# Four RMSNorms of a hybrid SSD/attention trunk: broadcasting 1/rms by a repeated column, scale-and-shift on ScalarE

## What is computed

```python
def rmsnorm(x, w):
    y = xf * lax.rsqrt(jnp.mean(xf * xf, axis=-1, keepdims=True) + EPS)
    return (y * w.astype(jnp.float32)).astype(x.dtype)

def modulate(h, shift, scale):
    return h * (1 + scale) + shift

a_lat = modulate(rmsnorm(x_lat, norm1_w[i]), sh1, sc1)
a_ctx = modulate(rmsnorm(x_ctx, norm1_w[i]), csh1, csc1)
```

## Time and profile before

| | |
|---|---|
| median of 3 runs | 1397.04 us (1394.56 to 1397.6) |
| the profiled execution, first to last instruction | 1395.9 us |
| TensorE busy (matmul) | 1232.0 us, 88%, 7274 instructions |
| TensorE weight load | 743.7 us, 53% |
| VectorE busy | 928.7 us, 67%, 1445 instructions |
| ScalarE busy | 581.8 us, 42%, 1005 instructions |
| GpSimd busy | 116.5 us, 8% |
| HBM read | 171.22 MB, 123 GB/s over the span |
| bodies of the norms n=0, 2, 3, 4 | from 44.7, 613.7, 973.3 and 1205.1 us, together about 64 us |

### The profile page before, as it was taken

One profiled execution on the slowest core, in us unless ns is written; L12 is line 12 of the kernel. 1 busy time (PEld: TensorE's weight loads), 2 busy tenths in 40 slices (PEclk: granted clock), 3 DMA queues, 4 the chain that ended last, 5 costly groups with the idle time before them and its releaser, 6 DMA issues.

```text
span 1395.9 us, 20639 instructions
## 1 busy us (share of the span) xinstructions
PE 1232.0 (88%) x7274; PEld 743.7 (53%) x7274; DVE 928.7 (67%) x1445; ACT 581.8 (42%) x1005; POOL 116.5 (8%) x127
## 2 busy tenths in 40 slices
PE   7679988988988768969999999997999977799997
PEld 7335554554554543424444444443765535688886
DVE  5984674674665568988788788564527755755654
ACT  2344543553653434323433333222334544456642
POOL 0003024014015110000000000000000000000000
PEclk9989989989989969979999999998999997899998
DMA  9213102202202033634564554522222100355552
GB/s 391 89 56 106 61 16 92 73 15 79 86 31 91 1 121 112 225 145 181 183 238 183 187 227 155 218 85 89 91 91 91 60 30 31 122 212 207 181 196 106
DMA packets 24957, 172.88 MB, mean 124 GB/s; under 512 B 2768, under 2 KB 2768, under 8 KB 6608
## 3 DMA queue, kind: packets, MB, share of 16 engines
q1 hardware_dynamic: 19008, 129.28, 25.4%
q0 software_dynamic: 5184, 37.75, 7.4%
q10 hardware_dynamic: 720, 5.24, 1.0%
HBM read 171.22 MB, written 1.05 MB: 123 GB/s over the span
## 4 chain that ended last, share of the span: by engine, by line
PE 49%; DVE 10%; issue 2%; ACT 2%; DMA 0%; DVEq 0%; ACTq 0%; POOL 0%; SPq 0%
PE bank L1284 14%; PE bank L1285 14%; PE bank L1286 14%; PE bank L1569 1%; DVE arena L756 1%; DVE arena L803 1%; PE bank L1583 1%; DVE arena L798 1%; PE bank L1556 1%; PE bank L1558 1%; PE bank L1557 1%; ACT wh L390 1%; DVE arena L1014 1%; DVE hl L794 1%; PE bank L1576 1%
## 5 line engine op out<-in xcount | busy, mean ns | idle before, releaser
L1284 PE MATMUL bank<-hh,wh 128*128 128x512 f16 (+1 forms) x1152 | 399.8, 347 | 38.4 <-DVE hl L794 19.3
L726 DVE SCALAR_TENSOR_TENSOR wl<-raw,wh 128x1024 f16<-128x1024 f32 (+1 forms) x232 | 269.0, 1177 | 237.5 <-ACT wh L390 235.5
L1285 PE MATMUL bank<-hl,wh 128*128 128x512 f16 (+1 forms) x1152 | 399.2, 347 | 0.0
L1286 PE MATMUL bank<-hh,wl 128*128 128x512 f16 (+1 forms) x1152 | 398.8, 346 | 0.0
L390 ACT ACTIVATE wh<-raw 128x1024 f16<-128x1024 f32 (+1 forms) x232 | 229.9, 1011 | 288.8 <-PE bank L1286 219.1
L1284 PEld LDWEIGHTS bank<-hh,wh 128*128 128x128 f16 x1152 | 114.8, 100 | 147.8 <-issue 62.0
L1284 PE MATMUL bank<-arena,wh 128*128 128x512 f16 (+1 forms) x544 | 182.0, 335 | 10.9 <-DVE wl L726 3.8
L1285 PE MATMUL bank<-arena,wh 128*128 128x512 f16 (+1 forms) x544 | 181.9, 334 | 0.0
L1286 PE MATMUL bank<-arena,wl 128*128 128x512 f16 (+1 forms) x544 | 181.8, 334 | 0.0
L756 DVE SCALAR_TENSOR_TENSOR arena<-arena,araw 128x1024 bf16<-128x1024 f32 x144 | 167.6, 1219 | 0.2
L1286 PEld LDWEIGHTS bank<-hh,wl 128*128 128x128 f16 x1152 | 114.3, 99 | 95.7 <-issue 6.6
(11 more groups left out here) (194 smaller groups left out, 1451.5 us busy)
## 6 DMA issues: line engine op xcount, KB each, us to landing
raw<-wgu SPq DMA_DIRECT2D x44, 1024.0 KB, 4.8
arena<-wadaT POOLq DMA_DIRECT2D x36, 1024.0 KB, 5.1
raw<-wdn SPq DMA_DIRECT2D x16, 896.0 KB, 4.6
raw<-wxg SPq DMA_DIRECT2D x8, 1024.0 KB, 4.8
raw<-wz SPq DMA_DIRECT2D x8, 1024.0 KB, 4.8
raw<-wout SPq DMA_DIRECT2D x8, 1024.0 KB, 4.8
raw<-wdn SPq DMA_DIRECT2D x8, 1024.0 KB, 4.8
raw<-wqk SPq DMA_DIRECT2D x8, 1024.0 KB, 4.8
```

Source lines behind the costliest of these rows:

```text
L726: ve.scalar_tensor_tensor(wl[:, u.slot, a:b], raw[:, u.slot, a:b], WS, wh[:, u.slot, a:b], ALU.mult, ALU.subtract).then_inc(lo_done, 1)
L1284: pe.matmul(o, wh[:, u.slot, wsl], ahi[:, k, t0:t1], start=st, stop=False)
L1285: pe.matmul(o, wh[:, u.slot, wsl], alo[:, k, t0:t1], start=False, stop=False)
L1286: i = pe.matmul(o, wl[:, u.slot, wsl], ahi[:, k, t0:t1], start=False, stop=en)
```

## The change

Four things are changed.

1. `bcast` multiplies, for each block of 128 tokens, the column of `rt` repeated 128 times (as the weights) with the identity. The result is the same: 1/rms of each token on all partitions. It waits for c_rr; the matrices `rdg`, the semaphore c_dg and the product on VectorE are gone. `acc` keeps the memory.
2. `root` first issues a Sqrt of one element (eps into an unused column), ahead of its wait for the sums.
3. The scale-and-shift is issued by ScalarE as `Identity` with the columns wsc and wsh as scale and bias, for chunk k ahead of the rounding of chunk k-1. VectorE keeps the multiply for chunk k and the subtraction, which is now for chunk k-2.
4. In n=1 VectorE's small product for the gate column stands ahead of the reciprocal instead of behind it.

```diff
             def root(n, width, cs):
 
+                act.activation(small[:, 1:2], eps, ACT.Sqrt)
                 act.wait_ge(c_ss, n + 1)
                 act.activation(rt[:, cs:4], OB[0][:, cs:4], ACT.Sqrt, scale=1.0 / width, bias=eps).then_inc(c_rt, 1)
...
             def h_hi(n, t0):
 
-                for k in range(KC):
-                    act.wait_ge(n32_ok, HN[n] * KC + k + 1)
-                    act.activation(hh[:, k, t0:T], n32[:, k % 2, t0:T], ACT.Copy).then_inc(hh_ok, 1)
+                m = HN[n] * KC
+                kinds = [(0, 0, TC), (1, TC, T)][t0 // TC:]
+                for k in range(KC + 1):
+                    if k < KC:
+                        act.wait_ge(nt_ok, m + k + 1)
+                        if k >= 2:
+                            act.wait_ge(h_ok, m + k - 1)
+                        for b, a, e in kinds:
+                            i = act.activation(n32[:, k % 2, a:e], nt[:, k % 2, a:e], ACT.Identity, scale=wsc[:, k, b:b + 1],
+                                               bias=wsh[:, k, b:b + 1])
+                        i.then_inc(n32_ok, 1)
+                    if k:
+                        act.wait_ge(n32_ok, m + k)
+                        act.activation(hh[:, k - 1, t0:T], n32[:, (k - 1) % 2, t0:T], ACT.Copy).then_inc(hh_ok, 1)
...
                 ve.reciprocal(rt[:, cs:4], rt[:, cs:4]).then_inc(c_rr, 1)
-                ve.wait_ge(c_rr, n + 1)
-                ve.tensor_tensor(rdg[:, cs * P:T].rearrange("p (c l) -> p c l", l=P),
-                                 ident[:, None, :].to_broadcast([P, 4 - cs, P]),
-                                 rt[:, cs:4][:, :, None].to_broadcast([P, 4 - cs, P]), ALU.mult).then_inc(c_dg, 1)
...
             def h_lo(n, t0):
...
                 ve.wait_ge(c_bc, n + 1)
-                for k in range(KC):
-                    ve.tensor_tensor(nt[:, k % 2, t0:T], x[:, k, t0:T], OB[1][:, t0:T], ALU.mult).then_inc(nt_ok, 1)
-                    ve.wait_ge(nt_ok, m + k + 1)
+                for k in range(KC + 2):
+                    if k < KC:
+                        if k >= 2:
+                            ve.wait_ge(n32_ok, m + k - 1)
+                        ve.tensor_tensor(nt[:, k % 2, t0:T], x[:, k, t0:T], OB[1][:, t0:T], ALU.mult).then_inc(nt_ok, 1)
                     if k >= 2:
-                        ve.wait_ge(h_ok, m + k - 1)
-                    for b, a, e in kinds:
-                        i = ve.tensor_scalar(n32[:, k % 2, a:e], nt[:, k % 2, a:e], wsc[:, k, b:b + 1], wsh[:, k, b:b + 1],
-                                             ALU.mult, ALU.add)
-                    i.then_inc(n32_ok, 1)
-                    if k:
-                        lo(k - 1)
-                lo(KC - 1)
+                        ve.wait_ge(hh_ok, m + k - 1)
+                        ve.tensor_tensor(hl[:, k - 2, t0:T], n32[:, k % 2, t0:T], hh[:, k - 2, t0:T], ALU.subtract).then_inc(h_ok, 1)
...
-            inverse(1, 0)
             gw = small[:, 16:32]
             step(ve.tensor_scalar(gw, cc("gnw"), AS, None, ALU.mult))
+            inverse(1, 0)
...
             def bcast(n, cs):
 
-                pe.wait_ge(c_dg, n + 1)
-                pe.matmul(OB[1][:, cs * P:T], ones, rdg[:, cs * P:T], start=True, stop=True).then_inc(c_bc, 1)
+                pe.wait_ge(c_rr, n + 1)
+                for c in range(cs, 4):
+                    i = pe.matmul(OB[1][:, c * P:(c + 1) * P], rt[:, c:c + 1].to_broadcast([P, P]), ident, start=True, stop=True)
+                i.then_inc(c_bc, 1)
```

More of the change, by code:

```diff
@@ L157, in build @@
         n32 = carve(2 * T).rearrange("p (b t) -> p b t", b=2)
-        rdg = carve(T)
+        acc = carve(T)
         mark = at[0]
@@ L170, in build @@
         pre = carve(2 * 520).rearrange("p (b s t) -> p b s t", b=2, s=2)
-        acc = rdg
         xbc = carve(6 * T).rearrange("p (q t) -> p q t", q=6)
@@ L268, in build @@
         sqd, ssd = sem("sqd"), sem("ssd")
-        c_ss, c_rt, c_rr, c_dg, c_bc = [sem(n) for n in ("c_ss", "c_rt", "c_rr", "c_dg", "c_bc")]
+        c_ss, c_rt, c_rr, c_bc = [sem(n) for n in ("c_ss", "c_rt", "c_rr", "c_bc")]
         nt_ok, n32_ok, hh_ok, h_ok = sem("nt_ok"), sem("n32_ok"), sem("hh_ok"), sem("h_ok")
@@ L405, in ada_load @@
                 act.dma_start(araw[:, :], wada[a]).then_inc(araw_in, 16)
-            def root(n, width, cs):
-                act.wait_ge(c_ss, n + 1)
-                act.activation(rt[:, cs:4], OB[0][:, cs:4], ACT.Sqrt, scale=1.0 / width, bias=eps).then_inc(c_rt, 1)
             def square_pair(n, k, t0, up):
@@ L418, in square_pair, with root @@
                     act.activation(sq[:, m, None, t0:T], x[:, bass.ds(k + m, 1), t0:T], ACT.Square).then_inc(sqd, 1)
+            def root(n, width, cs):
+                act.activation(small[:, 1:2], eps, ACT.Sqrt)
+                act.wait_ge(c_ss, n + 1)
+                act.activation(rt[:, cs:4], OB[0][:, cs:4], ACT.Sqrt, scale=1.0 / width, bias=eps).then_inc(c_rt, 1)
             def h_hi(n, t0):
-                for k in range(KC):
-                    act.wait_ge(n32_ok, HN[n] * KC + k + 1)
-                    act.activation(hh[:, k, t0:T], n32[:, k % 2, t0:T], ACT.Copy).then_inc(hh_ok, 1)
+                m = HN[n] * KC
[12 more added lines that the diff above has]
+                        act.activation(hh[:, k - 1, t0:T], n32[:, (k - 1) % 2, t0:T], ACT.Copy).then_inc(hh_ok, 1)
             def evac_pre(u, g, tile, b):
@@ L789, in h_lo @@
                 m = HN[n] * KC
[L790 to L794, removed]
                 ve.wait_ge(c_bc, n + 1)
-                for k in range(KC):
-                    ve.tensor_tensor(nt[:, k % 2, t0:T], x[:, k, t0:T], OB[1][:, t0:T], ALU.mult).then_inc(nt_ok, 1)
-                    ve.wait_ge(nt_ok, m + k + 1)
-                    if k >= 2:
-                        ve.wait_ge(h_ok, m + k - 1)
-                    for b, a, e in kinds:
-                        i = ve.tensor_scalar(n32[:, k % 2, a:e], nt[:, k % 2, a:e], wsc[:, k, b:b + 1], wsh[:, k, b:b + 1],
-                                             ALU.mult, ALU.add)
-                    i.then_inc(n32_ok, 1)
-                    if k:
-                        lo(k - 1)
-                lo(KC - 1)
+                for k in range(KC + 2):
[3 more added lines that the diff above has]
+                        ve.tensor_tensor(nt[:, k % 2, t0:T], x[:, k, t0:T], OB[1][:, t0:T], ALU.mult).then_inc(nt_ok, 1)
+                    if k >= 2:
+                        ve.wait_ge(hh_ok, m + k - 1)
+                        ve.tensor_tensor(hl[:, k - 2, t0:T], n32[:, k % 2, t0:T], hh[:, k - 2, t0:T], ALU.subtract).then_inc(h_ok, 1)
             def residual(k, banks, t0):
@@ L1292, in _, with ssum @@
             H = (hh, hl)
-            def ssum(n, cs):
+            def ssum(cs):
                 for c in range(cs, 4):
@@ L1328, in _ @@
                     pe.wait_ge(ssd, KC)
-                    ssum(0, 0)
+                    ssum(0)
             i.then_inc(a0_mm, 1)
@@ L1500, in _ @@
             pe.wait_ge(ssd, SQ_G + 16)
-            ssum(1, 0)
+            ssum(0)
             bcast(1, 0)
@@ L1534, in norm @@
                 pe.wait_ge(ssd, sums)
-                ssum(n, cs)
+                ssum(cs)
                 bcast(n, cs)
```

## The result

| | before | after |
|---|---|---|
| median of the runs | 1395.97 us (1394.56 to 1397.6, 4 runs) | 1404.7 us (1399.92 to 1405.18, 4 runs) |
| ratio | | 1.0056, 95% interval 1.0035 to 1.0077 |
| the profiled execution | 1395.9 us | 1398.3 us |
| TensorE, VectorE, ScalarE busy | 1232, 929, 582 us | 1228, 907, 610 us |

The changed kernel is slower by 8.7 us between the medians, about 7.8 by the ratio. The forecast was 1404.5. The profiled execution of the changed kernel is the fastest of its four; the other three have spans of 1402.9 to 1403.5 us. So the two profiles differ by 2.4 us only, and the change has to be read inside the stages, not from the spans. Where the rest of the difference went is told under "What was not expected".

The account below looks back on a forecast made before the run. The prediction took TensorE's waits for the stages making hh and hl (n=0, 2, 3, 4) as the bound. Its terms summed to +7.5 us, put on the median of 1397.04: 1404.5 us, range 1398.5 to 1411.

Parts of the forecast that it names:

- Rival D: Whole kernel: the waiting is made up elsewhere, time within 2 us of before, 1397 us; chance 0.06.
- seventh hl after the first multiply: Norm body at 512 columns: hl of the seventh chunk ready at 18.41 us against 15.24, 3.17 us later.
- n=2 and n=3, each: Norms of 512 columns: 3.17 us lost by the later seventh hl, 0.85 gained by the broadcast, +2.32 us each.
- n=0: Norm of 512 columns: 3.17 us lost by the later seventh hl, 0.61 gained by the dropped product, +2.56 us.
- n=4: Norm of 256 columns: 2.12 us lost by the later seventh chunk, 0.60 gained by the broadcast, +1.52 us.
- n=1, n=5: Gated and final norm, using only the broadcast: -0.65 us (0.85 gained, 0.2 lost to the early Sqrt) and -0.60 us.
- The ring: Norm bodies: ScalarE's shift and copy and VectorE's subtraction wait in turn, never overlapping; period 2.39 us against 1.97.
- The broadcast: Norm heads: dropped product and four smaller matmuls gain 0.85 us at 512 columns, 0.61 in n=0, 0.60 at 256.
- TensorE's idle time: TensorE's matmuls waiting on the subtraction that makes hl: idle time up by 8 to 10 us.
- rival C: TensorE's clock falls low in n=2 and n=3, about 3 us each, 1 us in n=4: 1411 us; chance 0.10.
- The early Sqrt: Norm heads: no gain from bringing the table load forward; about 0.2 us of ScalarE, delaying n=1 by that.
- The tables: ScalarE in the norm bodies: no reload between Identity and Copy; otherwise 16 loads of 1.28 us a stage, some 80 us.

Follow-up runs that it names:

- e4: The changed kernel with ScalarE rounding chunk k right after its own shift of chunk k, not one chunk later: 1385.79 us, ratio 0.9932.
- e5: The changed kernel with three buffers instead of two for the shifted chunk, order kept: 1388.39 us, ratio 0.9940.
- e8: The changed kernel without the early Sqrt of one element: 1400.6 us in one execution.
- e2: The kernel before with the new broadcast alone, scale-and-shift still on VectorE and no early Sqrt: 1390.16 us, ratio 0.9965.
- e1: The changed kernel run once more with no edit: 1404.06 us, ratio 1.0051 to the kernel before.

## Why the prediction was right

Its sign, its mechanism and its size held: +7.5 us forecast, +7.8 by the ratio. That 1404.5 and 1404.7 lie only 0.2 us apart is luck: the forecast stood on 1397.04, the median of three runs of the kernel before, and that of four is 1395.97. Rival D, that the waiting is made up elsewhere, would have left the time where it was; the interval of the ratio begins at 4.9 us. The single terms show small errors that partly point the same way.

| | forecast | measured |
|---|---|---|
| start of the broadcast after the reciprocal, gain | 0.73 us | 0.73 |
| four fp32 matmuls instead of one, gain | 0.12 | 0.00 |
| shift, start to start, two halves | 1.00 | 0.99 |
| period in n=2 | 2.39 | 2.43 |
| seventh hl after the first multiply | 18.41 | 18.62 |
| n=2 and n=3, each | +2.32 | +2.66 |
| n=0 | +2.56 | +2.61 |
| n=4 | +1.52 | +1.96 |
| n=1, n=5 | -0.65, -0.60 | -0.56, -0.48 |
| sum | +7.5 | +8.9 |

*The ring.* In the body above it is 0.99 (shift to copy) + 0.65 (copy to subtraction) + 0.79 (subtraction to shift) = 2.43 us. The prediction had 1.00 + 0.66 + 0.73. The term that was too small is the hop from VectorE to ScalarE's shift: 614.45 to 614.56, 0.11 us (0.10 in the turn above), where 0.04 was read from the earlier trace rows, between VectorE's scale-and-shift and ScalarE's copy. Six turns make it 0.2 us in each stage, and e4 and e5, which only cut the loop, show that the loop was the cause.

*The broadcast.* The product's 0.73 us was right to the hundredth. The matmul was mis-sized: eight records of 128x128 take 2.08 us, exactly as the two of 512 columns did. The price of 1.96 came from the transposes; 2.08 lies above both of the bounds named, 1.87 and 1.97. At 256 columns it is the same:

```profile
1204.56 1.22 PE L1302 MATMUL bank<-kp,small 128*128 128x128 f32 x4 [1.30 <-DVE small L788]
1205.82 0.75 DVE L803 TENSOR_TENSOR arena<-x,bank 128x256 f32<-128x256 f32 x2 [1.31 <-PE bank L1302]
...
1216.96 0.28 PE L1282 MATMUL bank<-hh,wh 128*128 128x256 f16 x1 [0.63 <-DVE hl L806]
```

1.22 us as in the earlier trace rows, so the gain is 0.46, not 0.60. The seventh chunk starts 1216.96-1205.82 = 11.14 us after the first multiply (forecast 10.84), with a period of 1.46 for 1.41. That hop and the matmul make n=4 the term with the largest error, 0.44 us.

*TensorE's idle time.* "Up by 8 to 10 us" seems refuted by the page's group, 19.3 to 24.8. But the matmuls of n=3 have another line (L1556), where the wait for hl went from 5.2 to 8.1 us (0.95+1.03+0.87+0.94 us ahead of the last four chunks that waited, 4.32 ahead of the first). Together it is 5.5+2.9 = 8.4.

*n=0.* Its seven waits for hl sum to 12.2 us before and 12.3 after, and still the stage ends 2.6 us later. All of its matmuls now last about 0.6 us, where most of the third to sixth chunks' were 0.39 before: the time between chunks is filled by slower matmuls. The third chunk's first matmul, before and after:

```profile
52.14 0.39 PE L1284 MATMUL bank<-hh,wh 128*128 128x512 f16 x1 [0.51 <-DVE hl L794]
```

```profile
52.91 0.61 PE L1282 MATMUL bank<-hh,wh 128*128 128x512 f16 x1 [0.97 <-DVE hl L806]
```

This is what rival C feared, in the one stage where it costs nothing, as TensorE had the time. In n=2, 3 and 4 the late matmuls stayed at 0.38 and 0.28 us, so C did not come about there.

*The early Sqrt.* No gain, as forecast; its cost in n=1 is 0.1 us and not 0.2. *The gate column.* Moving it ahead of the reciprocal in n=1 was put at nothing and brings nothing: from the start of the table load to the first instruction of the body on VectorE it takes 4.09 us in e8, which has the move, and 4.02 in e2, which doesn't. *The tables.* No load stands between Identity and Copy, as the Trainium skill (ScalarE: Activation LUTs, section Table sets: the hidden batching unit) has it; the number of loads is that of the kernel before.

The sum by the stages is +8.9 us, and by the two measured ratios it is +7.8 and +7.1 with intervals of about 3 us on either side. That the forecast of 7.5 lies nearer to the ratios than 8.9 does is chance: the terms were too small by 1.4 us, and the measurement can't tell the two.

## What to carry to other kernels

Before a step is moved to an engine that has time, write down for each instruction which one it waits for, including the one that frees its buffer, and follow the arrows round: if copy, subtraction and next shift lie on one closed loop, their times add up even where both engines are idle for part of every turn, and one more buffer or another order on one queue opens it. Here that was worth 18 us, more than either half of the change moved. And measure the halves of a change apart: one gained 0.35% and the other lost 0.82%.

## What was not expected of the hardware

The 32 small fp32 matmuls of a modulation unit inside the scan (two columns each) last 7 us in some executions and 4 in others, with the same kernel. The timelines of the kernel before, of the changed kernel, and of the changed kernel in e1:

```profile
488.18 6.96 PE L1311 MATMUL bank<-s,araw 128*128 128x2 f32 x32 [0.93 <-DVE arena L940]
```

```profile
489.03 4.01 PE L1311 MATMUL bank<-s,araw 128*128 128x2 f32 x32 [0.93 <-DVE arena L938]
```

```profile
491.03 6.96 PE L1311 MATMUL bank<-s,araw 128*128 128x2 f32 x32 [0.93 <-DVE arena L938]
```

Of the eleven profiles here six have 6.96 us in this place and five have 3.94 to 4.31. The granted clock (the share of the full clock that TensorE was given) over these matmuls is 0.50, the low level of 1.2 GHz, in the first and the third, and 1.00, the high level of 2.4 GHz, in the second until 492.3 us. The two executions of one and the same kernel are 0.8 us apart at 454 us and 4.9 us at about 500. It fits that two of e1's eight executions took 1398.9 us, at a mean granted clock of 0.949, and the other six 1403.9 to 1405.6, at 0.943 to 0.944. What puts this stretch on one level or the other stays open.

So the profiled execution of the changed kernel got 3 us there that the kernel before did not get, and this is nearly half of why the two spans differ by 2.4 us where the stages give 8.9. The rest can be placed too. VectorE's 232 weight conversions (wl) come in the same order in every trace; how much later one starts than in the kernel before is:

| start in the kernel before, us | changed kernel | changed kernel in e1 |
|---|---|---|
| 86.2 | +2.0 | +2.8 |
| 389.0 | +0.6 | +2.8 |
| 536.7, behind n=1 | -2.7 | +2.3 |
| 648.4, behind n=2 | +0.1 | +5.1 |
| 953.4 | +0.1 | +5.1 |
| 1009.8, behind n=3 | +2.4 | +8.2 |
| 1111.1 | +2.6 | +8.4 |
| 1180.5 | +0.2 | +6.3 |
| 1246.6, behind n=4 | +3.2 | +8.0 |
| the span | +2.4 | +6.8 |

In e1 the steps at the norms are about what the stages say, and between them nearly all of it stays, apart from 2.1 us between 1111 and 1180 us, where none of the six norms is. The execution profiled first loses 2.5 us there as well, and another 1.4 between 86 and 389 us. Why these stretches are shorter was not pinned down.

A trap in reading the clock: in n=0 of the changed kernel the matmuls of 512 columns last 0.61 to 0.63 us and start 0.43 us apart, as at the low level in n=2, and yet the granted clock of that stretch reads 1.00. The trace has no entry for the clock ahead of 65.6 us (51.7 in the kernel before), and a stretch without an entry reads as full. So the changed kernel ran all of n=0 at the low level, while the kernel before had the high one from 51.7 to 58.5 us. Near the start of a trace the length of a matmul is the safer reading of the two.
